# Sums of low halves on GpSimd in place of three of TensorE's products in the stick-breaking tails

## The reference

```
z              = q . k / 8
log_one_minus  = log_sigmoid(-z), 0 where s >= t
tail[s]        = sum over s' > s of log_one_minus[s']
a[s]           = exp(log_sigmoid(z[s]) + tail[s])
out            = sum over s of a[s] v[s]
```

## Time and profile before

| | us |
|---|---|
| three timed runs | 1357.34, 1354.95, 1356.29; median 1356.29 |
| profiled execution, its own time | 1352.88 |
| its span, from the first to the last instruction | 1351.0 |
| TensorE matmul busy | 1316.7 (97%) |
| VectorE busy | 749.1 (55%) |
| ScalarE busy | 623.2 (46%) |
| GpSimd busy | 281.7 (21%) |

### The profile page before, as it was taken

One profiled execution on the slowest core, in us unless ns is written; L12 is line 12 of the kernel. 1 busy time (PEld: TensorE's weight loads), 2 busy tenths in 40 slices (PEclk: granted clock), 3 DMA queues, 4 the chain that ended last, 5 costly groups with the idle time before them and its releaser, 6 DMA issues. The chain is left out here.

```text
span 1351.0 us, 18281 instructions
## 1 busy us (share of the span) xinstructions
PE 1316.7 (97%) x6494; PEld 1095.1 (81%) x6494; DVE 749.1 (55%) x1236; ACT 623.2 (46%) x1108; POOL 281.7 (21%) x343
## 2 busy tenths in 40 slices
PE   7999999999999999999999999999999999999997
PEld 6889777788888888888888878888888888878876
DVE  5444688833752235788444643336467237578734
ACT  5335867622532234898244423424334224346534
POOL 1201853100000006674000000000000000677510
PEclk9999999999999999999999999999999999999999
DMA  5423200022222232001232323331333322311111
GB/s 189 114 67 98 79 1 0 0 84 104 94 93 95 94 94 81 29 0 32 96 105 91 95 82 95 104 98 50 95 105 105 110 94 63 110 44 35 36 59 63
DMA packets 63515, 104.05 MB, mean 77 GB/s; under 512 B 3428, under 2 KB 21080, under 8 KB 63320
## 3 DMA queue, kind: packets, MB, share of 16 engines
q1 hardware_dynamic: 62384, 99.44, 22.6%
q0 software_dynamic: 944, 3.65, 0.9%
q10 hardware_dynamic: 120, 0.05, 0.0%
HBM read 101.03 MB, written 2.10 MB: 76 GB/s over the span
## 5 line engine op out<-in xcount | busy, mean ns | idle before, releaser
L1529 DVE TENSOR_TENSOR w_lo<-stage,w_hi 128x1024 fp32r<-128x1024 f32 (+4 forms) x188 | 223.1, 1187 | 455.9 <-ACT w_hi L1015 455.8
L1015 ACT ACTIVATE w_hi<-stage 128x1024 fp32r<-128x1024 f32 (+4 forms) x188 | 191.8, 1020 | 474.9 <-PE ps L469 474.2
L467 PE MATMUL ps<-a0h,w_hi 128*128 128x512 f32 x448 | 177.3, 396 | 2.7 <-DVE q_lo L2059 2.7
L469 PE MATMUL ps<-a0h,w_lo 128*128 128x512 f32 x448 | 174.8, 390 | 0.0
L468 PE MATMUL ps<-a0l,w_hi 128*128 128x512 f32 x448 | 174.7, 390 | 0.0
L2131 POOL TENSOR_TENSOR small<-small 128x16 f32<-128x16 f32 (+2 forms) x15 | 33.4, 2225 | 503.6 <-DVE small L1607 359.3
L467 PEld LDWEIGHTS ps<-a0h,w_hi 128*128 128x128 f32 x448 | 84.4, 188 | 21.8 <-issue 4.4
L467 PE MATMUL ps<-w_hi,a0h 128*128 128x512 f32 x256 | 101.2, 395 | 0.0
L467 PE MATMUL ps<-a1h,w_hi 128*128 128x512 f32 x256 | 99.9, 390 | 0.3 <-DVE w_lo L1529 0.3
L469 PE MATMUL ps<-w_hi,a0l 128*128 128x512 f32 x256 | 99.7, 389 | 0.0
L469 PE MATMUL ps<-a1h,w_lo 128*128 128x512 f32 x256 | 99.6, 389 | 0.0
(11 more groups left out here) (313 smaller groups left out, 2977.7 us busy)
## 6 DMA issues: line engine op xcount, KB each, us to landing
stage<-in_a_w_in SPq DMA_DIRECT2D x48, 512.0 KB, 3.7
stage<-in_ple_w_gate SPq DMA_DIRECT2D x16, 512.0 KB, 3.2
stage<-in_w_kv_shared SPq DMA_DIRECT2D x16, 512.0 KB, 3.5
stage<-in_sb_w_in SPq DMA_DIRECT2D x16, 512.0 KB, 3.5
stage<-in_a_w_out SPq DMA_DIRECT2D x16, 512.0 KB, 3.2
stage<-in_b_w_in SPq DMA_DIRECT2D x16, 512.0 KB, 3.8
stage<-in_mla_w_in SPq DMA_DIRECT2D x8, 512.0 KB, 3.6
stage<-in_mla_w_out SPq DMA_DIRECT2D x8, 512.0 KB, 3.2
```

The lines of the kernel that those rows point to most:

```text
L467: pe.matmul(bank, wh, mh, start=start, stop=False)
L469: return pe.matmul(bank, wl, mh, start=False, stop=stop)
L1015: act.activation(slab(w_hi[r % 2], L, nk, w), slab(stage[r % 4], L, nk, w), ACT.Copy).then_inc(S("hi_ready"), 1)
L1529: dve.tensor_tensor(slab(w_lo[r % 2], L, nk, w), slab(stage[r % 4], L, nk, w), slab(w_hi[r % 2], L, nk, w), ALU.subtract)\
```

## The change

For heads 2 to 15, three of the low products of later key blocks are replaced. Write l(k, q) for the low half of key block k in the columns of query block q. GpSimd makes three tiles of 128x128: l(2,3)+l(3,3), l(1,2)+l(2,2), and l(1,3) plus the first. TensorE multiplies the matrix of minus ones by these:

- key block 1: before l(2) with 256 columns and l(3) with 128; now l(2,2) with 128 columns, and the first sum with 128.
- key block 0: before l(1) with 384, l(2) with 256 and l(3) with 128; now l(1,1) with 128, and the other two sums together with 256.
- key blocks 2 and 3, the high halves, and heads 0 and 1 stay as they are.

TensorE waits for the semaphore `low_sum` ahead of the last product of key block 1. The sums of head h stand in GpSimd's queue behind the split of head h+2; those of heads 14 and 15 stand behind the loop, ahead of the transfer of `ws_tok`. The tile `low_sum` is placed 10 KB behind `sgm0`, over `rstd`. In the diff, `link` waits for the completion of the instruction that it is given.

```diff
+    low_sum = put("low_sum", [P, 3 * P], 10, F32R, of=SGM)
...
+                own = T - j * P
+                product(neg_tri_r, part(sp_h, j, j, own), j, own)
+                t = product(neg_tri_r, part(sp_l, j, j, own), j, own, stop=j == MB - 1)
+                for k in range(j + 1, MB):
                     n = T - k * P
-                    to = ps[3 * s + b][:, c + (k - j) * P:c + (k - j) * P + n]
-                    w = neg_tri_r if k == j else neg_one_r
-                    pe.matmul(to, w[:, :], sp_h[:, KEY_COL[k]:KEY_COL[k] + n], start=False, stop=False, skip_group_check=True)
-                    t = pe.matmul(to, w[:, :], sp_l[:, KEY_COL[k]:KEY_COL[k] + n], start=False, stop=k == MB - 1, skip_group_check=True)
+                    product(neg_one_r, part(sp_h, k, k, n), k, n)
+                    if first or j == MB - 2:
+                        t = product(neg_one_r, part(sp_l, k, k, n), k, n, stop=k == MB - 1)
+                if j < MB - 2 and not first:
+                    product(neg_one_r, part(sp_l, j + 1, j + 1, P), j + 1, P)
+                    if j:
+                        pe.wait_ge(S("low_sum"), h - 1)
+                        t = product(neg_one_r, low_sum[:, 0:P], MB - 1, P, stop=True)
+                    else:
+                        t = product(neg_one_r, low_sum[:, P:3 * P], MB - 2, 2 * P, stop=True)
...
+        def low_sums(h, kq):
...
+            pool.wait_ge(S("sp_done"), 2 * h + 1)
+            pool.wait_ge(S("tail_done"), h)
+            pool.wait_ge(S("kq_ok"), kq)
+            link(pool.tensor_tensor(low_sum[:, 0:P], part(2, 3), part(3, 3), ALU.add))
+            pool.tensor_tensor(low_sum[:, P:2 * P], part(1, 2), part(2, 2), ALU.add)
+            pool.tensor_tensor(low_sum[:, 2 * P:3 * P], part(1, 3), low_sum[:, 0:P], ALU.add).then_inc(S("low_sum"), 1)
+            pool.wait_ge(S("low_sum"), h - 1)
...
             for s in range(2):
                 pool.wait_ge(S("z_done"), 4 * i + (2 * s - 2))
                 kq_parts(i, s, KQ)
+                low_sums(2 * i + (s - 2), 2 * i + (s + 1))
         link.end(PAIRS - 2)
+        for s in range(2):
+            low_sums(HEADS - 2 + s, HEADS)
```

More of the change, by code:

```diff
@@ L748, in sb_tails, with product, part @@
                 b, c = KEY_BANK[j]
+                bank = ps[3 * s + b]
+                def product(w, moving, q, n, stop=False):
+                    at = c + (q - j) * P
+                    return pe.matmul(bank[:, at:at + n], w[:, :], moving, start=False, stop=stop, skip_group_check=True)
+                def part(t, k, q, n):
+                    at = KEY_COL[k] + (q - k) * P
+                    return t[:, at:at + n]
                 if j in (0, MB - 1):
                     pe.wait_ge(S("sp_done"), 2 * h + (1 if j else 2))
-                for k in range(j, MB):
+                own = T - j * P
+                product(neg_tri_r, part(sp_h, j, j, own), j, own)
+                t = product(neg_tri_r, part(sp_l, j, j, own), j, own, stop=j == MB - 1)
+                for k in range(j + 1, MB):
                     n = T - k * P
-                    to = ps[3 * s + b][:, c + (k - j) * P:c + (k - j) * P + n]
-                    w = neg_tri_r if k == j else neg_one_r
-                    pe.matmul(to, w[:, :], sp_h[:, KEY_COL[k]:KEY_COL[k] + n], start=False, stop=False, skip_group_check=True)
-                    t = pe.matmul(to, w[:, :], sp_l[:, KEY_COL[k]:KEY_COL[k] + n], start=False, stop=k == MB - 1, skip_group_check=True)
+                    product(neg_one_r, part(sp_h, k, k, n), k, n)
[8 more added lines that the diff above has]
+                        t = product(neg_one_r, low_sum[:, P:3 * P], MB - 2, 2 * P, stop=True)
             t.then_inc(S("tail_done"), 1)
@@ L2240, in _, with part @@
         extra_input(1)
+        def low_sums(h, kq):
+            def part(k, q, n=P):
+                at = KEY_COL[k] + (q - k) * P
+                return sp_l[:, at:at + n]
+            pool.wait_ge(S("sp_done"), 2 * h + 1)
[5 more added lines that the diff above has]
+            pool.wait_ge(S("low_sum"), h - 1)
         pool.wait_ge(S("ring_used"), end_load("sb_q2"))
@@ L2243, in _ @@
         with pool.Fori(2, PAIRS) as i:
-            link.begin(i, 2, 2)
+            link.begin(i, 2, 4)
             for s in range(2):
```

## The result

The changed kernel takes 1363.71 us (median; 1361.3 to 1364.6), the kernel before beside it 1356.32 (1354.88 to 1357.34): a ratio of 1.0057, with a 95% interval of 1.0045 to 1.007, or 7.4 us slower. The forecast was 1366.6 in a range of 1359 to 1372.5. The profiled execution took 1361.3 us with a span of 1359.5, which is 8.5 more of span than before.

What follows compares the result with a forecast made beforehand. GpSimd's queue was taken to bound the changed loop at 7.81 us a head against 6.89, making +10.3 us: 1363.2 on the profiled scale, 1366.6 us for the median with the 3.4 offset. Range 1359 to 1372.5.

Steps and rivals of the forecast that it cites:

- GpSimd sets the pace: Stick-breaking loop: with the sums, GpSimd's in-order queue exceeds 6.89 us a head, and TensorE takes its period; chance 0.58.
- The period: GpSimd's time per head in the loop: 4.34 + 1.37 + 0.54 + 0.10 + 1.46 = 7.81 us, between 7.28 and 8.29.
- GpSimd's waits for itself: Three waits per head for GpSimd's own results, around the sums, at 0.18 us each: 0.54 us.
- the register work: GpSimd's address work for the next head, no longer in idle time: 0.1 us a head, an estimate.
- The sum of 10.3 us: Whole-kernel slowdown: block 0 of head 13 starts 10.4 us late, less small savings, plus 0.25 in head 15.
- The loss of 1.46 us: GpSimd's loss per head beside VectorE's two-SBUF-input operations: 2.6 us overlap at a rate of 0.56.
- 14 x 0.17 = 2.4 us is what could be seen: TensorE's visible saving from block 0's shorter products, 0.17 us a head in 14 heads.
- rival 2: GpSimd keeps up in the loop, period under 6.89; TensorE's savings of 2.4 to 3.2 us show, about 1353.5; chance 0.05.
- Rival 1: GpSimd bounds the loop but its loss does not grow: period 7.2 to 7.5, +4 to +7 us, about 1361; chance 0.22.
- rival 3: Break-even in the loop: period 6.9 to 7.1, delay up to 2.4 us set against the saving, 1355 to 1358; chance 0.09.
- Rival 4: VectorE's casts stop GpSimd as well: period 8.9, delay 22 us, 1378; chance 0.06.
- The issue of `ws_tok`: Transfer behind the last sums: issue moves to about 654, lands about 662, hidden before its first reader at some 674.

Runs made afterwards that it cites:

- four_adds: The changed kernel with a fourth 128x128 addition on GpSimd per head, into a tile nobody reads: 1370.21 us, ratio 1.0106 to the kernel before.
- two_sums: The changed kernel with one addition of 2x128 columns instead of three additions; block 0 multiplies l(1,3) itself: 1358.19 us, ratio 1.0020 to the kernel before.
- adds_alone: The kernel before plus three GpSimd additions of constant tiles per head, TensorE's products unchanged and waiting for no sum: 1360.75 us, ratio 1.0038 to the kernel before.
- pe_alone: The changed kernel without GpSimd's additions: TensorE has the changed products, the sums tile is zeros: 1355.57 us, ratio 0.9995 to the kernel before.
- before_light: The kernel before with VectorE's low-half subtraction replaced by a copy of z (low halves wrong): 1353.87 us, ratio 0.9983 to the kernel before.
- two_sums_q: two_sums with GpSimd's two 256-column subtractions for the low queries made one of 512: 1363.18 us, ratio 1.0040 to the kernel before.
- before_late: The kernel before with one more GpSimd wait: the split starts after VectorE's low half of block 0: 1354.24 us, ratio 0.9988 to the kernel before.

## Why the prediction was right, and where it wasn't

**GpSimd sets the pace: right.** The forecast asked for a timeline with no gap over 0.2 us, a wait row for `low_sum` some 12 times and 1 us each, and more idle time on ScalarE and VectorE. Measured: no wait for others in the loop but a gap of 0.49 us in every second head, 13 times 0.85 us, ScalarE 1.38 us and VectorE 0.41 us less busy in 15. four_adds makes it causal: one addition more costs nearly its own time in every head.

**The period: 7.81 forecast, 7.61 measured.** By its terms, over the two heads from 573.90 on: two pairs of subtractions at 1.73 and 2.04 to 2.06 instead of 4 x 0.72 = 2.88, a loss of 0.90; sums of 1.77 and 2.20 instead of 1.37, 0.61 on the mean; casts at 0.61, nothing. The loss is 1.5 and was forecast at 1.46. GpSimd's waits for itself were put at 0.54 and the register work at 0.10; they are 0.08 before the sums, 0.08 at the link, and 0.17 and 0.49 in turn behind the last sum: 0.49 together. This is the term that was mis-sized, by 0.15 us. The remaining 0.05 to 0.1 lies in records that overlap by some hundredths.

**The sum of 10.3 us: 8.4 measured in the profile.** Eleven heads of 0.2 us less are 2.2. Block 0 of head 13 starts at 636.86 instead of the forecast 639.0, and all behind it follows. For the median another 1.0 goes: the profiled execution of the kernel before lies 3.4 us under its median, that of the changed kernel 2.4 under its own. (Of 83 executions of the kernel before, those with a mean granted clock of 0.997 took 1352.5 to 1353.5 us, those with 0.993 to 0.996 took 1354.4 to 1357.8.) So 7.4 us in the medians, 1363.71 against 1366.6; within the forecast's own range.

**The loss of 1.46 us: the size came out, the mechanism didn't.** The forecast put all of GpSimd's loss down to VectorE's operations with two SBUF inputs, at a rate of 0.56 of the overlap, and let the casts of GpSimd become longer. Those casts became shorter, both at their best (0.61), since GpSimd's order against VectorE's shifted; the loss moved to the subtractions and sums. VectorE's casts, which have one input, take part as well (single line: count, shortest/median/longest ns; then VectorE's timeline):
```profile
L1905 DVE CAST sp_h<-sp x32: 427/886/1032, 528.4 to 648.1; 128x768 fp32r<-128x768 f32 x16, 128x512 fp32r<-128x512 f32 x16
```
```profile
580.72 0.94 DVE L1905 CAST sp_h<-sp 128x512 fp32r<-128x512 f32 x1
581.69 0.83 DVE L1906 TENSOR_TENSOR sp_l<-sp,sp_h 128x512 fp32r<-128x512 f32 x1
582.45 0.94 DVE L1824 TENSOR_TENSOR a0l<-tmp,a0h 128x512 f32 x1
...
585.34 1.02 DVE L1905 CAST sp_h<-sp 128x768 fp32r<-128x768 f32 x1
586.40 1.37 DVE L1906 TENSOR_TENSOR sp_l<-sp,sp_h 128x768 fp32r<-128x768 f32 x1
```
Set beside GpSimd's timeline above, these rows show no common rate but turns. GpSimd's subtraction of the queries ends at 581.37, and the cast that began beside it at 581.66. GpSimd's first sum ends at 581.97, VectorE's low half at 582.52, GpSimd's second sum at 582.83, the output's low half at 583.39, the third sum at 583.70. Each ends behind the other engine's by its own shortest time less 0.12 to 0.15 us (0.43, 0.69, 0.46, 0.68 and 0.46 are the shortest). So what an overlap costs depends on who began first and how much it had left. Counted over ten heads by the operation of VectorE that GpSimd ended behind, it loses 1.57 us a head: 0.97 by the low half, 0.39 by the casts and 0.22 by the output's low half (1.51 above is less the hundredths by which records overlap). In the kernel before it was 1.0: 0.47, 0.43 and 0.10. The forecast read the casts' 0.43 as loss by two-input operations, and the rate that it took, midway between two readings, met the new sum in part by luck.

The Trainium skill, GPSIMD Engine Reference, Specifications, names a 2-port mode of VectorE as the second cause of contention. No row shows the mode in which a cast runs; that VectorE's casts from one SBUF input meet GpSimd here, 0.94 us instead of 0.43, agrees with it. While GpSimd holds the pace, what VectorE loses costs nothing; in two_sums, and in adds_alone before head 8, it does.

**"14 x 0.17 = 2.4 us is what could be seen": wrong.** That price of a saving on TensorE, and with it rival 2's 1353.5, rested on TensorE's 14.9 of 15 us. pe_alone shows 0.8 us with an interval that holds zero and ends at 2.2, and before_light why: the chain over VectorE is equally long, and only without it do the products count. The forecast itself took 0.34 us of this term, so nothing of the error went into the result. But had GpSimd kept up, the forecast of a gain would have been wrong. The view named two close limits ("TensorE's own work, and the chain"), and the step that failed was to price a cut of one of them as if the other had room.

**Rivals.** Rival 1 put the period at 7.2 to 7.5 and the time at about 1361: its mechanism, VectorE's operations falling on GpSimd's waits, isn't what is seen, and its upper end is 0.1 short. Its time of about 1361 is only 2.7 us under the result, so that the two weren't far apart as forecasts. Rivals 2 and 3 are out by the wait rows. Rival 4 was right that VectorE's casts hold GpSimd up, and wrong in the size: it added 1.08 us a head, where the casts cost 0.39 and had cost 0.43 before the change, inside the 0.93 that the forecast started from. The forecast's argument against it, that the subtraction explains the 0.29 us at 582.95, fails: that pair of GpSimd's ends at 584.68, ahead of VectorE's subtraction that began beside it at 584.12, and that one, at 1.36 us where its shortest is 0.96, was itself the one to wait.

**The issue of `ws_tok`: right that it costs nothing.** It starts at 650.0, 4 us ahead of the forecast's 654, lands 6.9 us later, and its first reader starts at 672.6:
```profile
L715 PE MATMUL ps<-cst,ws_tok x16: 272/273/273, 672.6 to 674.3; 128*128 128x128 f32 x16
L2290 POOL DMA_DIRECT2D ws_tok<-in_a_ws x1: 1185/1185/1185, 650.0 to 650.0; - x1
```

**Left open.** What in the turn of GpSimd's loop makes its wait for the last sum 0.49 instead of 0.17, and when TensorE's clock falls behind a wait and when it doesn't; the spread between executions goes with it.

## What to carry to other kernels

Before work is moved to an engine that looks idle on the page, count its period in the very loop that gets the work, with its waits for itself and what VectorE and GpSimd do to each other there: here 21% over the span was 74% in the loop, and 1.6 us of idle time a head had to take 1.37 us of additions that cost 2.5 with waits and contention. Look also at how long the single instructions are: one that holds the other engine up does so for all that it has left, as one subtraction of 512 columns in place of two of 256 did in two_sums_q's profile. An engine at 99% needn't be the bound: if a wait for a second chain recurs in the same loop, however short, shorten that chain first. The cheapest gain in this loop was one more wait, which kept GpSimd's casts away from the last step of VectorE's chain.

## What the runs showed of the hardware

**VectorE and GpSimd take turns.** From 551 to 645 us of the 14 profiles there are some 950 cases in which a cast, copy or two-input subtraction of VectorE and an operation of GpSimd overlap by more than 0.15 us. In all of them the one that began second ends a fixed time behind the other: VectorE's 128x512 subtraction 0.55 us (0.69 at its shortest), its 128x768 one 0.81 to 0.82 (0.96), its casts of 512 and 768 columns 0.28 to 0.29 and 0.41 to 0.42 (0.43 and 0.56); GpSimd's 128x128 addition 0.31 to 0.33 (0.46), its 64x256 subtraction 0.57 to 0.61 (0.72), its 64x512 cast 0.46 to 0.48 (0.61). That is its own shortest time less about 0.14 us, as if it ran only when the other is done. The 128x512 subtraction thereby takes 0.69 us with GpSimd held back (before_late), 0.83 behind a 128x128 sum, 0.98 behind a cast, and 1.11 behind a 128x256 sum. VectorE's operations that read one input from PSUM (lines 1881 and 1800) keep their 0.54 to 0.70 throughout.

**TensorE's clock after a wait.** In four_adds TensorE waits 1.72 us for a sum in head 6, and then the granted clock falls (stretches of 4 us, the clock is the third number from the end):
```profile
584.00:588.00 4.00, 2.28 (x17) 2.00 (x16) 3.74 (x6) 3.40 (x7) 3.68 (x7) 0.96 0.00 0
588.00:592.00 4.00, 4.00 (x12) 2.67 (x11) 2.74 (x4) 1.36 (x3) 3.76 (x5) 0.61 0.00 0
592.00:596.00 4.00, 4.00 (x31) 3.80 (x30) 2.43 (x4) 3.37 (x7) 3.36 (x6) 1.00 0.00 0
```
A mean of 0.61 lies between the two levels of 2.4 and 1.2 GHz, nearer to the lower. The values behind it take 3.28 us instead of 2.32:
```profile
589.17 3.28 PE L786 MATMUL ps<-a_T,v_pair 128*128 128x512 f32 x8
```
The two heads there take 16.94 us instead of 16.05, and the next two 15.92, so that some 0.8 of it stays lost. adds_alone has one such place, behind a wait of 1.66 us, and two_sums_q one, behind 2.3 us. It isn't certain to come: three other waits of 1.71 to 1.74 us in four_adds were followed by a clock of 1.00, as was one of 1.58 in adds_alone. The changed kernel's waits of up to 1.32 us left it at 1.00 throughout the loop.
